# One decoder layer with a mixture of experts on one core: the experts' rows dealt to and fro, weighted before they leave, and summed partly by accumulating DMAs

## What is computed

```python
def _moe(h, w_rg, b_rg, w_re, b_re, w_eg, w_eu, w_ed):
    p_group = jax.nn.softmax((hf @ w_rg + b_rg).astype(jnp.float32), axis=-1)
    g_star = jnp.argmax(p_group, axis=-1)
    p_sel = jnp.take_along_axis(p_group, g_star[:, None], axis=-1)
    ...
    top_v, top_i = lax.top_k(e_sel, TOP_K_IN_GROUP)
    w_top = jax.nn.softmax(top_v, axis=-1) * p_sel
    expert = g_star[:, None] * EXPERTS_PER_GROUP + top_i
    ...
    act = jax.nn.silu(a) * u * combine[:, sl, None]
    out = out + jnp.einsum('nef,efd->nd', act, w_ed[sl])
```

## Time and profile before

| | us |
|---|---|
| median of 3 runs (805.64 to 808.15) | 806.15 |
| the profiled execution | 805.87 |
| its span, first to last instruction | 804.0 |
| granted TensorE clock, mean share | 0.967 |
| PE busy | 723.4 (90%) |
| DVE busy | 340.9 (42%) |
| POOL busy | 82.9 (10%) |
| read from and written to HBM | 163.26 and 18.74 MB |

### The profile page before, as it was taken

The page is one execution under the profiler, slowest core; times in us unless marked ns, Lnnn a source line. Parts: engine busy times, 40 slices in busy tenths (PEclk is TensorE's granted clock), DMA queues, the critical chain, the costliest instruction groups (busy, mean ns, idle before and its releaser), DMA issues.

```text
span 804.0 us, 12356 instructions
## 1 busy us (share of the span) xinstructions
PE 723.4 (90%) x5112; PEld 538.4 (67%) x5112; DVE 340.9 (42%) x623; ACT 244.1 (30%) x489; POOL 82.9 (10%) x138
## 2 busy tenths in 40 slices
PE   5999999999999999999999999999988787878830
PEld 4888997678999998879999978864433232233310
DVE  6643358655546347343455523732223111111128
ACT  6234374643545333333122241311110010010013
POOL 3404000000000201000000011211112111111200
PEclk9999999999999999999999999999999899999975
DMA  8732111114221713432232299679999999999935
GB/s 315 225 106 62 54 53 53 54 53 136 63 65 53 280 63 144 171 89 83 74 85 93 91 355 386 239 261 398 416 419 418 419 415 404 415 411 419 401 146 220
DMA packets 82631, 173.02 MB, mean 215 GB/s; under 512 B 8064, under 2 KB 42208, under 8 KB 82560
## 3 DMA queue, kind: packets, MB, share of 16 engines
q1 hardware_dynamic: 72736, 148.52, 49.7%
q0 software_dynamic: 9840, 23.72, 7.9%
HBM read 163.26 MB, written 18.74 MB: 226 GB/s over the span
## 4 chain that ended last, share of the span: by engine, by line
PE 66%; DMA 11%; SPq 10%; DVE 8%; ACT 2%; issue 2%; POOLq 0%; ACTq 0%; DVEq 0%
PE bank L737 44%; DMA expert_down<-in_w_exp_down 9%; SPq L544 7%; PE bank L1189 5%; PE bank L1205 4%; SPq L549 2%; DVE w_split L1548 2%; ACT w_split L1243 1%; PE bank L757 1%; PE bank L1128 1%; PE bank L1114 1%; PE bank L1022 1%; PE bank L1028 1%; DVE s_state L1846 1%; DMA token_out<-token_out_scratch 1%
## 5 line engine op out<-in xcount | busy, mean ns | idle before, releaser
L737 PE MATMUL bank<-hT_split,w_split 128*128 128x272 f32 x1152 | 154.1, 292 | 0.0
L737 PEld LDWEIGHTS bank<-hT_split,w_split 128*128 128x128 f32 x1152 | 147.3, 188 | 2.1 <-issue 0.9
L737 PE MATMUL bank<-w_split,hT_split 128*128 128x512 f32 (+1 forms) x576 | 130.1, 380 | 0.5 <-DVE w_split L1548 0.5
L1189 PE MATMUL bank<-expert_gate_up,gatheredT 128*64 128x512 f32 x512 | 113.3, 593 | 3.7 <-DMA expert_gate_up<-in_w_exp_up 2.8
L737 PEld LDWEIGHTS bank<-w_split,hT_split 128*128 128x128 f32 x576 | 100.1, 188 | 22.9 <-issue 3.3
L1548 DVE TENSOR_TENSOR w_split<-w_raw,w_split 128x2048 fp32r<-128x2048 f32 (+1 forms) x35 | 75.9, 2168 | 83.1 <-ACT w_split L1243 83.1
L1205 PE MATMUL bank<-expert_down,expert_actT 128*64 128x512 f32 x256 | 69.6, 694 | 30.9 <-DMA expert_down<-in_w_exp_down 27.5
L1189 PEld LDWEIGHTS bank<-expert_gate_up,gatheredT 128*64 128x64 f32 x512 | 38.8, 137 | 75.0 <-issue 69.5
L1243 ACT ACTIVATE w_split<-w_raw 128x2048 fp32r<-128x2048 f32 (+1 forms) x35 | 63.4, 1812 | 42.4 <-PE bank L737 17.5
L1205 PEld LDWEIGHTS bank<-expert_down,expert_actT 128*64 128x64 f32 x256 | 20.9, 156 | 68.6 <-issue 38.7
L737 PE MATMUL bank<-gla_outT_split,w_split 128*128 128x272 f32 x384 | 49.4, 288 | 0.0
(11 more groups left out here) (355 smaller groups left out, 838.6 us busy)
## 6 DMA issues: line engine op xcount, KB each, us to landing
expert_gate_up<-in_w_exp_gate SPq DMA_DIRECT2D x64, 512.0 KB, 14.7
expert_gate_up<-in_w_exp_up SPq DMA_DIRECT2D x64, 512.0 KB, 15.7
expert_down<-in_w_exp_down SPq DMA_DIRECT2D x32, 1024.0 KB, 17.0
w_raw<-in_w_in SPq DMA_DIRECT2D x15, 1024.0 KB, 5.5
w_raw<-in_w_in SPq DMA_DIRECT2D x16, 512.0 KB, 4.7
s_state<-in_state_gla POOLq DMA_DIRECT2D x4, 1024.0 KB, 8.7
out_sample_gla_state<-s_state POOLq DMA_DIRECT2D x4, 1024.0 KB, 6.3
w_raw<-in_w_proj_gla SPq DMA_DIRECT2D x8, 512.0 KB, 4.2
```

Source lines behind the costliest of these rows:

```text
L737: ins = mm(out, stat(x, k), mov(y, k), start=first and n == 0 and m == 0, stop=last and n == len(ks) - 1 and m == 2)
L1189: ins = mm(P[2 + u][64 * half:64 * half + 64, :].rearrange("p (m n) -> p m n", m=2), XT[u][:, k, 64 * half:64 * half + 64], WGU[gb][:, k / ...
```

## The change

- **Dealing.** `slot_row` deals ranks to and fro over eight groups of eight partitions: ranks 0 to 7 to the first partition of groups 0 to 7, ranks 8 to 15 to the second partition of groups 7 to 0, and so on. Odd experts' ranks get 1,024 added in place of 64 (`ODD`), so that a rank over 63 matches no slot of either half by itself; the two steps that pushed such ranks out are gone.
- **First gathers.** They take their index column straight from the table; the two copies ahead are gone.
- **Weights per slot.** DVE splits the tokens' weights into three bf16 parts, spreads them over pairs, and PE makes a table of slot weights (a third part to `table_mm`), summed by `slot_weights` on DVE. POOL copies pair n's column (`WCOL`) at the head of `move_rows`; DVE's multiply of silu and up takes it as a scalar and waits for it (`columns`). The overflow parts get the same. Rows thus leave with their token's weight.
- **PE's keep_clock calls**: 13, 7, 12 before; 13, 5, 6 and 2 now, with the new table between the last two.
- **Tail.** POOL, when all scatters have landed, adds the first rows to `x_after_mix` in SBUF by five accumulating DMAs (semaphores `first_in`; blocks 3 and 4 share one and wait for both). SP loads the second rows alone. `add_experts` is one plain addition.
- The stores of the shifted windows count on `kv_stored` instead of a semaphore of their own.

```diff
@@ -25,7 +25,7 @@
 NFIX = NE // 2
-SPREAD, UNSPREAD = 39, 23
+ODD = 1024
 MAXOV = (2 * NTOK) // CAP + 3
@@ -63,14 +63,13 @@
     e = np.arange(NE)
-    parts["half_row"] = np.broadcast_to(CAP * (e % 2), (128, NE))
-    parts["half_end"] = np.broadcast_to(CAP + CAP * (e % 2), (128, NE))
+    parts["half_row"] = np.broadcast_to(ODD * (e % 2), (128, NE))
     parts["expert"] = np.broadcast_to(e, (128, NE))
...
     parts["pairsteps"] = np.broadcast_to(2 * np.arange(OVH // 2), (128, OVH // 2))
-    assert (SPREAD * UNSPREAD) % CAP == 1
-    parts["slot_row"] = np.broadcast_to(CAP * (p // CAP) + UNSPREAD * p % CAP, (128, 128))
+    group, lap = p % CAP // 8, p % 8
+    parts["slot_row"] = np.broadcast_to(ODD * (p // CAP) + 8 * lap + np.where(lap % 2, 7 - group, group), (128, 128))
     parts["over_pair"] = np.broadcast_to(np.arange(NFIX, NFIX + OVH), (128, OVH))
@@ -595,9 +601,7 @@
             for bl in range(NB):
-                for k in range(2):
-                    sp.dma_start(YI[2 * bl + k][0:rows(bl), :],
-                                 tok_d[k * NTOK + bl * 128:k * NTOK + bl * 128 + rows(bl), :]).then_inc(x_in[bl], 16)
+                sp.dma_start(YI[2 * bl + 1][0:rows(bl), :], tok_d[NTOK + bl * 128:NTOK + bl * 128 + rows(bl), :]).then_inc(x_in[bl], 16)
             for bl in range(NB):
@@ -629,7 +633,7 @@
             for name, src in (("sample_win_k", "cache_win_k"), ("sample_win_v", "cache_win_v")):
-                pool.dma_start(o[name][0, :, 0:WIN - DS], a[src][0, :, DS:WIN]).then_inc(win_stored, 16)
+                pool.dma_start(o[name][0, :, 0:WIN - DS], a[src][0, :, DS:WIN]).then_inc(kv_stored, 16)
             pool.dma_start(CK[:], a["cache_win_k"][0].rearrange("b s g d -> s b (g d)")).then_inc(cache_in, 16)
@@ -676,15 +680,13 @@
                 pool.indirect_dma_start(out=XG[u][:], out_offset=None, in_=h2_d,
-                                        in_offset=bass.IndirectOffsetOnAxis(ap=col[:], axis=0),
+                                        in_offset=bass.IndirectOffsetOnAxis(ap=col, axis=0),
                                         bounds_check=NTOK - 1, oob_is_err=False).then_inc(gathered[u], 16)
...
             for u in range(2):
-                pool.tensor_copy(ICG[u][:], IDXG[:, u:u + 1]).then_inc(columns, 1)
-            for u in range(2):
-                pool.wait_ge(columns, 3 + u)
-                gather(u, ICG[u])
-            pool.wait_ge(rows_ready, 2)
+                pool.sem_inc(columns, 1)
+                gather(u, IDXG[:, u:u + 1])
+            pool.wait_ge(rows_ready, 3)
 
@@ -692,12 +694,15 @@
                 pool.wait_ge(xg_turned, n + 2)
+                if not isinstance(n, int) or n:
+                    pool.wait_ge(act_done, n)
+                pool.tensor_copy(WCOL[u][:], column(WSLOT, n)).then_inc(columns, 1)
                 pool.tensor_copy(ICG[u][:], column(IDXG, n + 2)).then_inc(columns, 1)
...
                 pool.tensor_copy(ICS[u][:], column(IDXS, n)).then_inc(columns, 1)
-                pool.wait_ge(columns, 2 * n + 6)
+                pool.wait_ge(columns, 3 * n + 7)
                 pool.sem_inc(pool_passed, 1)
-                gather(u, ICG[u])
+                gather(u, ICG[u][:])
                 pool.wait_ge(y_out_a, n + 2)
@@ -716,13 +721,16 @@
                 pool.wait_ge(gathered[u], 16 * turns + 16)
+                pool.wait_ge(scattered[u], 16 * turns + 16)
             pool.sem_inc(pool_passed, 1)
+            for bl in range(NB):
+                pool.dma_start(X2[0:rows(bl), bl, :], tok_d[bl * 128:bl * 128 + rows(bl), :],
+                               accum_op=ALU.add).then_inc(first_in[min(bl, 3)], 16)
 
...
             pool.wait_ge(pstate_stored, 16)
-            pool.wait_ge(kv_stored, 16 * (2 + 2 * DB))
-            pool.wait_ge(win_stored, 32)
+            pool.wait_ge(kv_stored, 16 * (4 + 2 * DB))
 
@@ -1142,7 +1150,7 @@
             ins.then_inc(rank_mm, 1)
-            keep_clock(7)
+            keep_clock(5)
 
@@ -1165,7 +1173,10 @@
             pe.wait_ge(lg_out, NB)
-            keep_clock(12)
+            keep_clock(6)
+            pe.wait_ge(digits_ready, 2)
+            slot_table(P[7][:, 0:3 * NFIX], OHR, OHP[:, :, 0:3, :], range(2 * NB)).then_inc(table_mm, 1)
+            keep_clock(2)
             pe.wait_ge(gathered[0], 16)
@@ -1211,7 +1222,8 @@
                         pe.wait_ge(over_hot, 1)
-                        slot_table(P[5][:, 256:256 + 4 * OVH], OROW, ODIG, range(2 * NB)).then_inc(over_mm, 1)
+                        slot_table(P[5][:, 256:256 + 4 * OVH], OROW, ODIG, range(2 * NB))
+                        slot_table(P[5][:, 256 + 4 * OVH:256 + 7 * OVH], OROW, OWGT, range(2 * NB)).then_inc(over_mm, 1)
             pe.wait_ge(iters_ready, 2)
@@ -1972,9 +1984,7 @@
             ranks = P[4][:, 0:160].rearrange("p (b e) -> p b e", b=NB)
-            link(V.tensor_tensor(tmp, ranks, per_expert(cst("half_end")), ALU.is_ge))
-            link(V.scalar_tensor_tensor(out=sent, in0=tmp, scalar=1000.0, in1=ranks, op0=ALU.mult, op1=ALU.add))
-            chosen(R2["fixed"], sent, PROD)
+            chosen(R2["fixed"], ranks, PROD)
 
@@ -2005,7 +2015,25 @@
             link(V.tensor_tensor(R1["w1"][:], R1["w1"][:], R1["psel"][:], ALU.mult))
-            link(V.tensor_tensor(R1["w2"][:], R1["w1"][:], R1["e2"][:], ALU.mult))
+            V.tensor_copy(WTOK[:, 0:NB], R1["w1"][:])
+            link(V.tensor_tensor(WTOK[:, NB:2 * NB], R1["w1"][:], R1["e2"][:], ALU.mult))
+
+            def spread_weights(out, pairs, n):
+                return V.tensor_tensor(out, pairs[:].unsqueeze(2).to_broadcast([128, 2 * NB, 3, n]),
+                                       WPART[:].unsqueeze(3).to_broadcast([128, 2 * NB, 3, n]), ALU.mult)
+
+            def slot_weights(out, table, n):
+                link(V.tensor_copy(out, table[:, 0:n]))
+                link(V.tensor_tensor(out, out, table[:, n:2 * n], ALU.add))
+                return V.tensor_tensor(out, out, table[:, 2 * n:3 * n], ALU.add)
+
+            link(V.tensor_copy(WPART[:, :, 0], WTOK[:]))
+            link(V.tensor_tensor(WREST[:], WTOK[:], WPART[:, :, 0], ALU.subtract))
+            link(V.tensor_copy(WPART[:, :, 1], WREST[:]))
+            link(V.tensor_tensor(WREST[:], WREST[:], WPART[:, :, 1], ALU.subtract))
+            link(V.tensor_copy(WPART[:, :, 2], WREST[:]))
+            spread_weights(OHP[:, :, 0:3, :], PAIRH, NFIX).then_inc(digits_ready, 1)
+            V.memset(WSLOT[:, NFIX + OVH:NPC], 0.0)
 
@@ -2037,6 +2065,7 @@
                 link(spread_digits(ODIG, OPAIR, OVH))
+                link(spread_weights(OWGT[:], OPAIR, OVH))
                 row_onehot(OROW, R2["row"], slice(0, 2 * NB)).then_inc(over_hot, 1)
@@ -2061,6 +2090,7 @@
                 link(row_numbers(IDXG[:, cols], IF1[:, cols], table, 0, OVH))
+                link(slot_weights(WSLOT[:, cols], P[5][:, 256 + 4 * OVH:256 + 7 * OVH], OVH))
                 row_numbers(IDXS[:, cols], IF2[:, cols], table, 2, OVH).then_inc(over_ready, 1)
@@ -2070,14 +2100,18 @@
             dve.sem_inc(act_done, 1)
+            dve.wait_ge(table_mm, 2)
+            slot_weights(WSLOT[:, 0:NFIX], P[7], NFIX).then_inc(rows_ready, 1)
             dve.wait_ge(xg_turned, 2)
...
                 n = 2 * i + u
+                dve.wait_ge(columns, 3 * n + 5)
                 dve.wait_ge(silu_done, n + 1)
                 dve.wait_ge(act_turned, n + 1)
-                V.tensor_tensor(AC[u][:], SA[:], P[2 + u][:, FF:2 * FF], ALU.mult).then_inc(act_done, 1)
+                V.scalar_tensor_tensor(out=AC[u][:], in0=P[2 + u][:, FF:2 * FF], scalar=WCOL[u][:], in1=SA[:],
+                                       op0=ALU.mult, op1=ALU.mult).then_inc(act_done, 1)
                 dve.wait_ge(act_turned, n + 2)
@@ -2102,12 +2136,9 @@
                 n = rows(bl)
-                y1, y2 = YI[2 * bl], YI[2 * bl + 1]
-                dve.wait_ge(x_in[bl], 16 + 32)
-                link(V.scalar_tensor_tensor(out=y1[0:n, :], in0=y1[0:n, :], scalar=R1["w1"][0:n, bl:bl + 1], in1=X2[0:n, bl, :],
-                                            op0=ALU.mult, op1=ALU.add))
-                V.scalar_tensor_tensor(out=y1[0:n, :], in0=y2[0:n, :], scalar=R1["w2"][0:n, bl:bl + 1], in1=y1[0:n, :],
-                                       op0=ALU.mult, op1=ALU.add).then_inc(x3_ready, 1)
+                dve.wait_ge(x_in[bl], 16 + 16)
+                dve.wait_ge(first_in[min(bl, 3)], 16 if bl < 3 else 32)
+                V.tensor_tensor(YI[2 * bl][0:n, :], YI[2 * bl + 1][0:n, :], X2[0:n, bl, :], ALU.add).then_inc(x3_ready, 1)
 
```

More of the change, by code:

```diff
@@ L192, in decoder_step @@
     T0 = W0 + 20480
-    RR = [at(f"route_{n}", [128, NB, NE], F, T0 + 640 * n) for n in range(3)]
+    RR = [at(f"route_{n}", [128, NB, NE], F, T0 + 640 * n) for n in range(2)]
     PROD = at("route_products", [128, 2, NB, NE], F, T0 + 1920)
@@ L204, in decoder_step @@
     CMP = at("over_compare", [128, NE * 8], F, V0 + 5280)
+    OWGT = at("over_weight_parts", [128, 2 * NB, 3, OVH], BF, V0 + 6304)
```

(14 more changed lines are left out.)

## The result

The changed kernel took **826.2 us** (median of 4 runs, 823.1 to 828.4), the kernel before 805.9 beside it: a ratio of 1.0243, 95% interval 1.0205 to 1.0281. It is slower by 2.4%, where 802.3 was forecast and 795.5 to 809.5 allowed. The execution profiled is one of 826.02 us with a span of 824.2.

The account below looks back on a forecast made before the run. The expert stage was taken to wait for weights, bound by DMA engines with two late. Dealing -4.4, routing -0.65 and tail +1.2 sum to -3.85 on 805.87, 802.0; with 0.28 for the median, 802.3 us, range 795.5 to 809.5.

Parts of the forecast that it names:

- The dealing's term: Weights stage: the fullest DMA engine goes from 160 to 132 rows at 0.157 us each, -4.4 us.
- that is the idle time found above, with two engines late, so I take this map: Weights stage: 85 engine-us of missing rows matched some 84 idle, so an engine serves eight neighbouring partitions.
- map F: Gathers and scatters: a DMA engine serves four neighbouring partitions at two places 32 apart; rival 3's map, chance 0.07.
- Rival 3: Weights stage: under map F the new dealing puts 230 rows on the fullest engines, 13.2 us longer, 819.9; chance 0.07.
- The stage ends with its slowest engine: Weights stage: the fullest DMA engine's rows set the end, so 28 fewer rows give -4.4 us.
- Routing: Start: shorter DVE chain and earlier first gather, PE turning rows at 532.1 instead of 532.80, -0.65 us.
- Per pair: Expert pairs: POOL's column copy, DVE's scalar multiply and the merged window semaphore are covered, 0 us.
- Tail: After the last scatter: less DVE work, but accumulates counted as two reads; 28.5 against 27.3, +1.2 us.
- f = 1: Tail: an accumulated row costs the engines f times a plain row; at 1 the tail is 5.3 us less.
- Rival 1: Tail: accumulates cost the plain load price, tail -4.1 us, total 797.0; chance 0.27.
- rival 2: Tail: accumulates cost three times a plain load, total 807.6; chance 0.13.
- the chance of faster: Whole kernel: under 803.7 us, from rival 1 and three quarters of the forecast's case (0.44), stated as 0.58.

Follow-up runs that it names:

- run 2: The kernel before with only the new to-and-fro dealing over eight groups of eight partitions: 825.76 us, 1.0246 of the kernel before.
- run 4: The kernel before with only a dealing that is even over the engines of map F: 806.25 us, 1.0001 of the kernel before.
- runs 2 to 5 and 9: Run 2, run 4, run 5, run 9, and the changed kernel with a dealing even under map F: 808.62 us, 1.0035 of the kernel before.
- run 12: The kernel of run 4 with every scatter of an expert's rows repeated into a second scratch tensor: 817.61 us, 1.0143 of the kernel before.
- run 5: The kernel before with ranks in order (rank p mod 64 in partition p), no dealing: 809.7 us, 1.0044 of the kernel before.
- run 9: The kernel before with the to-and-fro dealing half levelled, half of the partitions exchanging half of their ranks: 813.02 us, 1.0094 of the kernel before.
- run 1: The changed kernel with the old dealing (rank 23p mod 64 in partition p), all else kept: 807.66 us, 1.0020 of the kernel before.
- run 6: The changed kernel with the old dealing and a tail without accumulates (SP loads both rows, DVE adds): 806.12 us, 1.0004 of the kernel before.
- run 7: The changed kernel, old dealing, POOL issuing plain loads instead of accumulates, first rows left out of the sum: 803.15 us, 0.9960 of the kernel before.

## Why the prediction was wrong

**The dealing's term: -4.4 us forecast, +19.7 measured** (run 2). The step that failed is "that is the idle time found above, with two engines late, so I take this map". I had 84 engine-us of idle time and chose the map whose missing rows made 85. The agreement was chance. The old dealing under map F has 146 and 143 rows on engines 0 and 8, so it too has two engines late; I had held against map F that it shows "no pair of engines so late". The idle time was taken to come from rows alone, which run 4 refutes: with even rows the dip in the middle windows stayed and was 1 to 3 GB/s deeper. A sum of idle time over 16 engines can't name a map, when other causes may be in it. The prices should have warned me: 13 us one way against 4 the other, for a rule that was given 0.07. "DMA: Bandwidth & Descriptors" of the Trainium skill (section "The descriptor swizzle") has map F for plain transfers of 128 partitions; runs 2 to 5 and 9 agree with it for indirect ones. Rival 3 was the case that came, with its sign (819.9), its mark (the share at half, 0.53 and 0.48, though from 776 to 782 and not from 750 on) and its mechanism.

**Its size.** Rival 3 put 84 x 0.157 = 13.2 us; measured was 19.7, or 0.23 us a row. An even row costs the plain price (run 12). So some 6 us are not in that price. Of these 0.4 stand behind the stage: the last scatter took 4.92 us from the copy ahead of it to the tail's first issue, in run 2 and in the changed kernel alike, against 4.54. The rest comes with the uneven load: the rate is down to 378 to 394 GB/s from the first window on, by packets that wait. Light engines that wait explain that rate, but not a longer stage; for this the heavy ones must have waited too or done more, and no record names the engine of a packet. This stays open. Nor does the count of the fullest engine alone set the cost: 38 rows more cost 3.5 us with two engines late (run 5) and 7.3 with eight (run 9), where the plain price says 6.0, and from 146 to 132 rows nothing came back. "The stage ends with its slowest engine" is a first guess, and no more.

**Routing: -0.65 forecast.** Its parts held. The gather was issued at 528.36 (528.1 forecast; in run 1 at 528.46), DVE's weights reached PE's second table at 530.63 (530.4). PE turned the first rows at 532.43 in run 1, a gain of 0.37, and at 533.10 with the new dealing: there the gather took 4.70 us from its issue, and PE waited for it 0.69 us. That wait was not in my sum; in run 1 it was 0.24. In the time nothing of it shows (run 6, which holds it together with the next term).

**Per pair: 0 forecast.** Run 6 holds it and the routing to -0.6 to +1.2 us together; no run separates them. DVE's multiply with a scalar takes 0.48 us, not 0.42, which shows in no time that was measured:

```profile
L2113 DVE SCALAR_TENSOR_TENSOR expert_act<-bank,slot_weight,expert_silu 128x256 f32<-128x256 f32 x16 | 7.7, 484 | 98.7 <-ACT expert_silu L1516 98.7
```

**Tail: +1.2 forecast, +1.0 in the trace** (+1.5 by runs 1 and 6). This term was right, with its mechanism. The last accumulate, block 4's, for which block 3 waits too, shows in the chain that ended last:

```profile
798.86 16.10 DMA x_after_mix<-token_out_scratch
```

It landed at 814.96, 19.0 us behind the first issue (19.3 forecast). I expected DVE to idle some us before block 3's addition. There it idled 0.29, and more before the first two: block 0's came 10.3 us behind the first issue, where it had been 4.9, and block 1's waited 2.15. The factor was 2.06 by the median packet and 1.85 by the shares, and at f = 1 the gain was 4.5, not 5.3. Rival 1 (plain price), at 0.27 the likeliest after the forecast, and rival 2 fall.

One slip besides: the chance of faster adds up to 0.60 (0.27 and three quarters of 0.44), not 0.58.

## What to carry to other kernels

Where rows move by indirect DMA beside a stream of weights, count rows per engine by the map before choosing who sits in which partition: here one table of 128 numbers was worth 20 us. When two maps fit a trace, price each when wrong, and run the table alone first. An accumulating DMA cost the engines about two loads here: give it only to what is needed last, and issue it behind the loads that are needed first.

## What was not expected of the hardware

- The map of four neighbouring partitions at two places 32 apart holds for gathers and scatters with indices, too. By it the fullest engine has 132, 146, 184 (two engines above 160), 184 (eight above 160) and 230 rows in the five dealings, and their medians are 806.3, 806.0, 809.7, 813.0 and 825.8 us. By eight neighbouring ones the dealings of 806.3 and 809.7 would have had 232 and 240 rows.
- The DMA share stays full while the rate is down, as a few long packets count as busy: share 1.00 to 1.01 at 378 to 390 GB/s, with a median packet of 159 ns all the while.
- POOL's records of accumulating DMAs are longer than those of plain ones, but they overlap. These rows of the profile after and of run 7 show it (minimum, median and maximum in ns, first and last start): 1,547 against 550 ns in the median (542 in the earlier trace rows), while the five starts stand within 2.3 us in both. So accumulates were issued as fast as loads.

```profile
L727 POOL DMA_DIRECT2D x_after_mix<-token_out_scratch x5: 973/1547/2170, 796.5 to 798.9; - x5
L726 POOL DMA_DIRECT2D token_out<-token_out_scratch x5: 522/550/567, 778.5 to 780.9; - x5
```
